# State-space groups: VectorE's two products of decay and scores each stand ahead of a modulation panel

## What is computed

```
seg   = cum[i] - cum[j]
decay = exp(where(causal, seg, -inf))
cb    = einsum('bign,bjgn->bgij', C_c, B_c)
y_intra = einsum('bgij,bghij,bjghp->bighp', cb, decay, x_c)
y_inter = einsum('bign,bghpn->bighp', C_c, state) * exp(cum)
y = y_intra + y_inter, then gated by silu(z) and normed by group
```

## Time and profile before

| | |
|---|---|
| median of 3 runs | 938.48 us (936.16 to 939.41) |
| profiled execution | 940.62 us, its span 938.9 us |
| mean granted TensorE clock | 0.992 |
| TensorE busy | 922.6 us |
| VectorE busy | 717.1 us |
| ScalarE busy | 546.7 us |
| GpSimd busy | 117.2 us |
| state-space groups in the trace | about 193 to 335 us |

### The profile page before, as it was taken

How to read it: one execution, slowest core, us unless ns; L and a number is a source line. 1 busy time by engine, 2 the same in 40 slices (tenths; PEclk the granted TensorE clock), 3 DMA queues, 4 the chain that set the end, 5 groups by cost and what they waited for, 6 DMA issues and landing times.

```text
span 938.9 us, 17275 instructions
## 1 busy us (share of the span) xinstructions
PE 922.6 (98%) x6692; PEld 849.0 (90%) x6692; DVE 717.1 (76%) x963; ACT 546.7 (58%) x760; POOL 117.2 (12%) x95
## 2 busy tenths in 40 slices
PE   8999999999999999999999999999999999999997
PEld 4799999999898989988888888999878999999885
DVE  4947788899999968568877556679876798877664
ACT  4366656666676575355655445567665676666442
POOL 0000200044744400010000001303100100000000
PEclk8999999999999999999999999999999999999999
DMA  9954555568767756645656565535433355655661
GB/s 337 360 183 136 180 179 181 182 226 245 222 221 234 244 192 208 191 140 159 201 184 196 185 197 181 164 109 189 134 103 112 113 182 198 189 187 184 194 210 45
DMA packets 85709, 175.53 MB, mean 187 GB/s; under 512 B 5441, under 2 KB 46801, under 8 KB 85649
## 3 DMA queue, kind: packets, MB, share of 16 engines
q1 hardware_dynamic: 84672, 172.39, 56.7%
q0 software_dynamic: 368, 1.31, 0.4%
q10 hardware_dynamic: 608, 1.00, 0.3%
HBM read 173.63 MB, written 1.05 MB: 186 GB/s over the span
## 4 chain that ended last, share of the span: by engine, by line
PE 81%; DVE 9%; DMA 4%; issue 3%; ACT 1%; DVEq 0%; SPq 0%; ACTq 0%
PE proj_ps L1651 17%; PE proj_ps L1634 14%; PE proj_ps L1635 14%; PE proj_ps L1636 14%; PE proj_ps L1654 9%; DVE mod_acc L952 5%; DMA raw<-in_panels 3%; DVE w_lo L940 2%; PE proj_ps L1694 1%; PE proj_ps L1695 1%; PE proj_ps L1696 1%; PE aux L2009 1%; PE aux L1722 1%; DMA mod_first<-in_panels 1%; PE aux L1730 1%
## 5 line engine op out<-in xcount | busy, mean ns | idle before, releaser
L940 DVE TENSOR_TENSOR w_lo<-raw,w_hi 128x1024 fp32r<-128x1024 f32 x276 | 347.8, 1273 | 126.8 <-ACT w_hi L473 126.1
L473 ACT CAST w_hi<-raw 128x1024 fp32r<-128x1024 f32 x276 | 286.6, 1047 | 196.6 <-PE proj_ps L1636 72.5
L1634 PE MATMUL proj_ps<-act_pair,w_hi 128*128 128x256 f32 x1024 | 292.3, 285 | 0.4 <-issue 0.4
L1635 PE MATMUL proj_ps<-act_pair,w_hi 128*128 128x256 f32 x1024 | 289.6, 283 | 0.0
L1636 PE MATMUL proj_ps<-act_pair,w_lo 128*128 128x256 f32 x1024 | 289.6, 283 | 0.0
L1634 PEld LDWEIGHTS proj_ps<-act_pair,w_hi 128*128 128x128 f32 x1024 | 196.2, 192 | 4.8 <-issue 2.7
L1635 PEld LDWEIGHTS proj_ps<-act_pair,w_hi 128*128 128x128 f32 x1024 | 196.3, 192 | 0.6
L1636 PEld LDWEIGHTS proj_ps<-act_pair,w_lo 128*128 128x128 f32 x1024 | 196.3, 192 | 0.0
L1651 PE MATMUL proj_ps<-act_pair,w_hi 128*128 128x512 f32 x256 | 69.9, 394 | 0.0
L1651 PE MATMUL proj_ps<-ff_pair,w_hi 128*128 128x512 f32 x256 | 69.9, 394 | 0.0
L437 POOL TENSOR_TENSOR tmp_b<-tmp_b 128x512 f32<-128x512 f32 x4 | 5.2, 1297 | 465.2 <-ACT tmp_b L496 465.2
(11 more groups left out here) (337 smaller groups left out, 1631.5 us busy)
## 6 DMA issues: line engine op xcount, KB each, us to landing
raw<-in_panels SPq DMA_DIRECT2D x308, 512.0 KB, 4.0
mod_first<-in_panels SPq DMA_DIRECT2D x16, 512.0 KB, 10.8
xres<-in_x_t SPq DMA_DIRECT2D x2, 512.0 KB, 6.0
out_t<-tmp_a SPq DMA_DIRECT2D x4, 256.0 KB, 2.2
wst<-in_ws_t POOLq DMA_DIRECT2D x1, 512.0 KB, 3.8
bs_sb<-in_bs_rows POOLq DMA_DIRECT2D x1, 512.0 KB, 4.5
level_sb<-in_levels ACTq DMA_DIRECT2D x1, 512.0 KB, 5.5
cols<-in_cols SPq DMA_DIRECT2D x1, 267.0 KB, 3.2
```

The source lines that it names most:

```text
L473: nc.scalar.copy(w_hi[:, s, :], raw[:, s, :]).then_inc(hi_done, 1)
L940: tt(out=w_lo[:, s, :], in0=raw[:, s, :], in1=w_hi[:, s, :].bitcast(F32), op=ALU.subtract).then_inc(taken, 1)
L1634: mm(dst, hi, xh, start=first and k == 0 and nt % 2 == 0, stop=False, skip_group_check=True)
L1635: mm(dst, hi, xl, start=False, stop=False, skip_group_check=True)
```

## The change

Inside the loop over the two chunks, the call that adds panel 2 + c to `mod_acc` moves from the front of the body to its end, behind the product of chunk c.

```
                 mod_panel_of(1)
                 for c in range(2):
-                    mod_panel_of(2 + c)
                     dve.wait_ge(S["decay_ok"], g * 2 + (c + 1))
                     dve.wait_ge(S["cbm_ok"], g + 1)
                     tt(out=decay[:, c], in0=decay[:, c], in1=spread(cbm[:, c], 1, HPG), op=ALU.mult).then_inc(S["m_ok"], 1)
+                    mod_panel_of(2 + c)
                 for s in range(2):
                     split_lo(g + (GROUP["zg"] + 2), s)
```

## The result

The changed kernel took 945.95 us (median of 6 runs, 943.53 to 947.74) against 938.71 us for the kernel before (6 runs). The ratio is 1.0083 with a 95% interval of 1.0069 to 1.0097, so +7.8 us where +4.2 was forecast (the two medians lie 7.2 us apart). The profiled execution took 947.74 us, span 946.0.

What follows compares the result with a forecast made beforehand. The prediction took the ring through slot 3, not TensorE's matmuls, as the bound. Lateness of L1212 summed over the groups to +3.7 to +6.7 us; it took +4.2, 942.7 us against the median, range 937 to 946.

Steps and rivals of the forecast that it cites:

- the likeliest case: State-space groups: the ring pays for the later release of slot 3, +2.8 to +6.7 us; chance 0.6.
- the sum: Lateness of the next L1212 added turn by turn: +3.7 us by group 7 at short X, about +6.7 with X as before.
- the ring: Groups' loop: panel 3 frees slot 3, weights land, w_hi, zg copy, SiLU, L1212, next panels; 18.0 us a turn, sets pace.
- (a): First product, L1866: d0 (product of chunk 0) ends one panel earlier, 2.2 us in group 3; alone gives TensorE 3.3 us.
- (b): Groups 0, 1, 6 and 7: the first product fills panel 2's waits for its tile, 2.1 us in all.
- (c): Two products, not one, ahead of panel 3 delay slot 3's release: 0.54 + 0.90 = 1.45 us beside GpSimd, 0.61 alone.
- m: Time from L1212 to the end of panel 3; 10.55 us in group 3 before, forecast about 12.0.
- (d): Loads of slots 2 and 3 share less of their flight, so X may shrink to 3.55 to 3.6 us.
- X: Time from slot 3's release to start of its w_hi; 3.5 to 3.6 us in four turns, 4.5 to 5.2 in three.
- The restart of TensorE: First yb panel after group 7: starts at 354 to 357 us, not 350.6, after a stop of 2 us or more.
- No difference: Rival: VectorE's own list sets the turn, a product costing 0.61 us; sum +0.3, 938.8 us; chance 0.27.
- Faster: Rival: TensorE is the bound, not the ring; the 3.3 us wait at L1866 goes, 935.2 us; chance 0.13.

Runs made afterwards that it cites:

- the two half-changes: Against the kernel before: only the first product moved ahead of panel 2, ratio 0.9998; only the second moved ahead of panel 3, ratio 1.0085.
- the cut on another engine, change_silu_early: Changed kernel with ScalarE's SiLU of z moved ahead of w_hi of slot 3: 935.85 us, ratio 0.9981 to the kernel before.
- first_only: Kernel before with only the first product moved, ahead of panel 2; the second stays behind panel 3: 937.85 us, ratio 0.9998.
- the pair of runs with a shorter GpSimd list: Kernel before and changed kernel, each with a_upto_lo in 4 of 128 columns in groups 1 to 7: 937.28 and 940.26 us.
- the second profile: Changed kernel run once more, unaltered: 945.10 us, ratio 1.0078 to the kernel before.
- both_before_last: Kernel before with only the second product moved, so panel 2 and both products stand ahead of panel 3: 945.35 us, ratio 1.0085.
- change_bridge: Changed kernel with three added matmuls of ones ahead of the sum of squares of group 7: 944.30 us, ratio 1.0086 to the kernel before.

## Why the prediction was right in its mechanism and too small in its size

The measured +7.8 us lies above the +2.8 to +6.7 of the likeliest case. The kind of loss and its way were forecast; two sizes in the sum were not.

**What bounded, and the ring.** Right. L1212 waits in all groups; the two half-changes, the cut on another engine and the turn's sum agree. The ring was forecast from the rows of the kernel before, and its sum holds after.

**(a) and the worth of TensorE's wait.** The wait is gone, as forecast, and alone it brought nothing (first_only). That the end of the groups swallows it is shown only in part, since that profile's clock fell too.

**(b) the landing waits.** Right: 2.1 to 0.3 us.

**(c) the price of a product ahead of panel 3.** m was forecast 12.03, 10.85, 11.9 and 10.8 us in groups 3 to 6, and is 11.97, 10.81, 11.94 and 10.79. The taking of turns, 0.54 + 0.90 us, is what these come from. It was read off the rows and holds in them; the pair of runs with a shorter GpSimd list did not test it. By the rule of the Trainium skill, "SBUF — State Buffer", section "Who interferes with whom", the one of the two engines that comes later stands until the other's instruction ends. The trace agrees: in group 1 it was the later starter of the two that took the longer time, whichever engine that was (the rows of both profiles above), and the first product of group 3, begun 0.47 us into GpSimd's c_in, ends only 0.55 us after it (254.33 against 253.78):

```profile
252.35 1.43 POOL L419 TENSOR_TENSOR c_in<-c_in,stg 128x512 f32<-128x512 f32 x1 [0.81 <-ACT c_in L662]
```

**(d) X.** Right for groups 0 to 6 in size: 3.55 to 3.67 us in each, no 4.5 or 5.2 left; in the second profile only group 0 had a longer one, 4.48. That the loads share less of their flight is the reason I gave; no run tried it.

**The step that failed is the sum, in two terms.** First "m +0.4" in group 1 and "m +1.35" in group 2 (with "+0.4" in group 0). Measured against before they are +1.07 and +2.09 (and +1.36) in the first profile; in the second they are +0.30, +2.09 and +0.26, so that only group 2's is there each time. The sum had let d0 run ahead of GpSimd in group 1; that is true of the second profile and false, by 0.12 us, of the first (the rows are shown above). For group 2 I had kept GpSimd's start where it was, 5.97 us after L1212. It came 4.64 us after it:

```profile
233.71 0.69 DVE L1195 TENSOR_TENSOR decay<-decay,cbm 128x512 f32<-128x512 f32 x1 [0.19 <-DVE mod_acc L952]
234.32 2.31 DVE L952 SCALAR_TENSOR_TENSOR mod_acc<-raw,silu_c,mod_acc 128x1024 f32<-128x1024 f32 x1
```

```profile
233.91 1.63 POOL L419 TENSOR_TENSOR c_in<-c_in,stg 128x512 f32<-128x512 f32 x1 [1.48 <-ACT c_in L662]
```

When L1212 is late and TensorE isn't, TensorE's cum matmul no longer holds c_in back. ScalarE's exponential of c_in in group 2 waited for it before and doesn't now:

```profile
233.67 0.60 ACT L662 ACTIVATE c_in<-aux 128x512 f32<-128x512 f32 x1 [1.21 <-PE aux L1855]
```

```profile
233.23 0.60 ACT L662 ACTIVATE c_in<-aux 128x512 f32<-128x512 f32 x1
```

So GpSimd begins while panel 2 still would have had VectorE to itself (2.31 us and not 1.28). The sizes for groups 4 and 6 came out right; that for group 2 did not. Second, "Group 7: m +0.55": m was right (9.37, +0.51), but I let X of group 7 be as before, 3.84 us, and it was 5.24 and 4.86. The w_hi of slot 3 in group 7:

```profile
338.75 1.04 ACT L473 CAST w_hi<-raw 128x1024 fp32r<-128x1024 f32 x1 [2.03 <-DMA raw<-in_panels]
```

Behind group 7 no modulation panel comes; SyncE issues loads of full weight panels as `w_lo` frees the slots. w_lo starts right behind panel 3 now and not behind a product, so the next load is issued 1.3 us after that of slot 3 and was 1.9 us before. I took this for the reason, but it can't be the whole of it. In both_before_last the next load follows as soon, 1.3 us, and X is only 4.04 us:

```profile
335.57 1.05 ACT L473 CAST w_hi<-raw 128x1024 fp32r<-128x1024 f32 x1 [1.56 <-DMA raw<-in_panels]
```

There the load of slot 2 had gone out 3.5 us ahead of that of slot 3, and in the changed kernel 1.9 us, as in the kernel before. The DMA engines weren't fuller either while the load of slot 3 was in flight: their share is 0.85 in the changed kernel (333.7 to 338.7 us) and 0.83 before (328.6 to 332.3 us). Why this landing is slow stays open. Counted as lateness of L1212 after the first panel of group 0, the sum was missed by 0.7 us in each of groups 0, 1 and 2 (0.4, 1.5 and 2.0 us late, where -0.3, 0.1 and -0.1 were forecast), by no more in groups 3 to 6, and by another 1.3 us in group 7. Together these are the 3.4 us by which L1212 of group 7 missed it in the first profile (7.1 us late against 3.7). In the second profile it is 5.5 us late and the miss is 1.8 us, of which 1.0 stands after group 2 and the rest comes in group 7; in change_bridge it is 6.6 us late. That the first profile had groups 0 and 1 at their longer size is chance, which the forecast did not allow for.

**The restart of TensorE** was forecast at 354 to 357 us with a longer stop. It came at 357.4 (355.4 in the second profile) and the stop was not there: TensorE had waited before, at `xdt`, `w_lo` and the sum of squares, and came late itself. A wait at L1872 for the state tile doesn't show either.

**The rivals.** "No difference" priced a product at 0.61 us; m shows 1.4 to 1.6 in groups 3 to 5, where no landing is covered. "Faster" needed a ring that isn't the bound; it comes true only when ScalarE's SiLU leaves the ring (0.9981 and 0.9951).

## What to carry to other kernels

A wait of the busiest engine is worth its length only if nothing longer closes behind it. Follow the buffer that the moved instruction frees, through landing and the next engines, back to the list it came from; where the ring binds, an instruction put ahead of the last release of a turn lengthens that turn by its whole price, and one moved to another place on the same side of that release cost nothing here (first_only). Behind the release it isn't free: with both products there TensorE's wait became the longer way, at 3.7 us. What an instruction costs beside another engine can hang on which of the two starts first, 0.06 us ahead or 0.12 us behind in one case here, so a sum of such prices has a width. Where such a ring binds, look for the engine in it that idles for a landing and let it do its later work there: that edit, with the first product alone moved, is 0.49% faster than the kernel before, while either alone gave nothing.

## What was not expected of the hardware

TensorE's granted clock falls to its lower level for about 3 us in some executions of one and the same kernel and not in others: four times in one profile of the changed kernel's groups, once in the next, never in the kernel before's. It fell twice in first_only as well, where TensorE had lost only 0.8 us to waits. In change_silu_early, where TensorE hardly waits in the groups (0.7 us by the weight loads for a product), it doesn't fall. The mean clock of the changed kernel's first six runs goes from 0.984 (947.74 us) to 0.994 (944.42 us), so part of the scatter between runs may be of this kind; it isn't all of it, since 945.04 us came at 0.988 and 947.58 us at 0.989. What starts such a fall was not settled.
